# A third buffer for one-hot tiles, eight gathered rows later, and other steps for two blocks' picks

## The chip, the cores and the metric

The kernel runs on one core of a Trainium2 chip. The metric is the device time of one launch in microseconds; three runs of the kernel before gave 2902.71, 2904.64 and 2911.29 us, so its median is 2904.64 us. The profiled execution took 2901.28 us.

## The reference, cut to what matters

A sequence of 512 tokens of width 1024 goes through two mixing layers and a third block. The last part of that block is the expert layer that the change touches:

```
s = einsum('thpc,hpnc->thpn', q, sub_keys)          # 8 heads, two halves of 128 keys
v1, i1 = top_k(s[:, :, 0], 16);  v2, i2 = top_k(s[:, :, 1], 16)
top_s, pos = top_k(v1[..., :, None] + v2[..., None, :], 16)   # of 256 sums
idx = take_along_axis(cand_idx, pos);  g = softmax(top_s)     # cand_idx = i1 * 128 + i2
a = einsum('thkd,td->thk', u[idx], x);  w = gelu(a) * g
out = einsum('thk,thkd->td', w, v[idx])              # u, v: 16384 experts x 1024
```

Every token takes 8 x 16 = 128 of 16384 experts, each with its own row of u and of v. After it comes a small gated projection, and the output is stored.

## The kernel before, in words

The 512 tokens are four blocks of 128. The expert layer is computed in two ways at the same time.

**Blocks 0 and 1, gathered.** There are 256 "rows": row r is one expert per token. GpSimd gathers the row of u (512 KB for 128 tokens) into one of four buffers (L1903), VectorE multiplies it with XN, the block's normalised rows, and sums (row_dot, L2552), ScalarE makes gelu times the softmax weight of it (L1689, L1691), GpSimd gathers the row of v (L1912), and VectorE adds it, weighted, to X (row_add, L2564). row_add(r - 8) follows row_dot(r) on VectorE and waits for the weight of row r - 8. XN holds both blocks, 4 KB per partition each: XN[:, 0] at 196 KiB, XN[:, 1] at 200 KiB. XN[:, 1] is read from row 128 on.

**Blocks 2 and 3, dense.** A loop over 128 steps g (TILES), written out by hand, multiplies the 256 tokens with all experts, 128 at a time. In step g TensorE computes tile_products(g + 1) (L1216) from a STREAM tile that SyncE loads into a ring of three (L623); ScalarE takes gelu of the products (L1734, and L1732 for the part whose gates are known). The gates of a token are a 128 x 128 table, built four tokens at a time ("quads", 64 of them) in steps 82 to 126, one or two per step: VectorE writes one-hot tiles (quad_ones, L2612) into ONE, which has two buffers, at 12 and 204 KiB; ScalarE scales one half of each by the softmax (scale_quad, L1741, four instructions); TensorE multiplies the halves (build_quad, L1234) into one of three banks; ScalarE keeps the columns of later steps (keep_quad, L1748), and VectorE multiplies the earlier ones into the products (quad_gates, L2621). tile_gates(g) (L2628, VectorE) multiplies gelu(g) with the gates that were already kept. After step 127 follow 128 tile_sums on TensorE (L1244), with further STREAM tiles, while the rest of the gathered rows goes on.

**The order in a step.** VectorE: a share of the routing (top-16 searches, one-hot picks), the "ahead" quad_ones of step g + 1, tile_gates(g), rows up to rows_by(g), quad_gates of step g, then the "behind" quad_ones of step g + 1. ScalarE: gelu(g), scale of the ahead quads, row weights up to weighed_by(g), keep_quad of step g, scale of the behind quads. Which quads are ahead is told by ones_ahead (L108): those whose buffer the quads built before step g have left. rows_by (L114) is 46 + 3(g + 1)/5 up to step 82 (95 rows there), then one row in two steps (117 at step 127). The engines are tied by semaphores alone and each runs its own list in order, so VectorE may be several steps behind ScalarE.

**Picks.** The routing of block 2 ends in VectorE's step 39, that of block 3 in step 73 (PICKED_2, PICKED_3 less one); it ends with soft_start (L2529). ScalarE takes the exponential in its step PICKED + 5 (L1708), VectorE divides by the sum in its step PICKED + 6 (soft_end, L2533 to L2535), TensorE transposes the picks in its step PICKED + 8 (L1225), ScalarE copies them in step PICKED + 9 (L1713). All waits are by semaphore.

**Around the loop.** Before the STREAM tiles SyncE stores SCORES[1] and two blocks of X to memory (L609, L611). After step 127 ScalarE issues the load of SCORES[1] into KEPT (L1825), which VectorE needs for the next piece of routing.

Of the kernel before, what the change touches and what calls it, by code (L numbers as in the profile page):

```python
# [14 lines left out]
P = 128  # L15
# [34 lines left out]
TILES = 128  # L50
STREAM_RING = 3
PICKED_2, PICKED_3 = 40, 74
SOFT_AFTER, SOFT_END, TURNED, TURNED_COPY = 5, 6, 8, 9
QUAD_FROM = 82
DENSE_HEADS = (2, 3, 0, 1)
ARENA = 215360
SCALE128 = float(128 ** -0.5)
# [49 lines left out]

def ones_ahead(g):  # L108

    free = quads_by(g - 1) + 2  # L110
    return [q for q in quads_of(g + 1) if q < free], [q for q in quads_of(g + 1) if q >= free]


def rows_by(g):  # L114

    if g < 0:
        return 46
    if g <= QUAD_FROM:
        return 46 + (g + 1) * 3 // 5
    return rows_by(QUAD_FROM) + (g - QUAD_FROM) // 2  # L120


def row_place(r):
# [96 lines left out]
def program(nc, x, xT, mem, wstream, fmvec, rows, norm_rows, consts, levels, subkeys, pT, proj, peer_u, peer_v,  # L220
            experts, out):
    with ExitStack() as ctx:
# [23 lines left out]
        HROWN = at("HROWN", [P, P], 204)  # L246

        STREAM = [at(f"STREAM{i}", [P, D], kib) for i, kib in enumerate((24, 28, 8))]
        ONE = [at("ONE0", [P, 2, 4, P], 12), at("ONE1", [P, 2, 4, P], 204)]
        XTD = at("XTD", [P, KD, 2 * P], 16)  # L250
        KEPT = at("KEPT", [P, 2048], 16)
        GD = at("GD", [P, 256 * P], 32)
# [250 lines left out]
        scores_back = sem("scores_back")  # L503
        x_spilled = sem("x_spilled")
        x_back = sem("x_back")
        unit_in = sem("unit_in")
        unit_exp = sem("unit_exp")
        unit_picked = sem("unit_picked")
# [70 lines left out]
                self.n, self.off = base + times * per, 0  # L579

        scores_kept = nc.dram_tensor("scores_kept", [P, 2048], F32, kind="Internal").ap()
        x_kept = nc.dram_tensor("x_kept", [P, 2, D], F32, kind="Internal").ap()

        block = ctx.enter_context(nc.Block())
# [2 lines left out]
        @block.sync  # L587
        def _(sp):
            for k in range(KD):
                sp.dma_start(XT[:, k, :], xT[k * P:(k + 1) * P, :]).then_inc(first_loaded[k], 16)  # L590
                sp.dma_start(W[:, 0, k * T:(k + 1) * T], wstream[0][:, k * T:(k + 1) * T]
                             ).then_inc(first_loaded[k] if k < KD - 1 else slot_loaded[0], 16)
            sp.dma_start(mem_tm.rearrange("p (b d) -> p b d", b=2),
                         mem.rearrange("(b p) d -> p b d", p=P)).then_inc(loaded_mem, 16)
            sp.dma_start(W[:, 1, :], wstream[1]).then_inc(slot_loaded[1], 16)
            sp.dma_start(V[:, :], fmvec).then_inc(loaded_const, 16)
            sp.dma_start(C[:, :], consts).then_inc(loaded_const, 16)
            sp.dma_start(HROWN[:, :], norm_rows[640:768].partition_broadcast(P)).then_inc(loaded_const, 16)
            sp.dma_start(X[:, :, :], x.rearrange("(b p) d -> p b d", p=P)).then_inc(loaded_x, 16)

            n = SLOTS["ple"]
            with sp.Fori(1, n // 2) as i:
                for s in range(2):
                    sp.wait_ge(slot_used, i * 2 + s - 1)
                    sp.dma_start(W[:, s, :], wstream[ds(i * 2 + s, 1)].rearrange("a p n -> (a p) n")
                                 ).then_inc(slot_loaded[s], 16)

            sp.wait_ge(sk_ready, 4)
            sp.dma_start(scores_kept, SCORES[1]).then_inc(scores_out, 16)  # L609
            sp.wait_ge(h_ready, 4)  # L610
            sp.dma_start(x_kept, X[:, 2:4, :]).then_inc(x_spilled, 16)  # L611

            sp.wait_ge(bank_full, POS["xT_f2"] + 2)
            for m in range(2 * TILES):
                if m == 2:
                    sp.wait_ge(x_spilled, 16)
                if m >= STREAM_RING:
                    last = m - STREAM_RING
                    if last < TILES:
                        sp.wait_ge(a_full, last + 1)  # L620
                    else:
                        sp.wait_ge(v_used, last + 1 - TILES)
                sp.dma_start(STREAM[m % STREAM_RING][:, :], experts[m]).then_inc(streamed[m % STREAM_RING], 16)  # L623

            for i, b in enumerate(PLE_ORDER):
                for half in range(2):
                    cols = slice(half * T, (half + 1) * T)
                    sp.wait_ge(y_ready, 2 * i + half + 1)
                    sp.dma_start(out[0, b * P:(b + 1) * P, cols], xb(b)[:, cols]).then_inc(stored, 16)
            sp.wait_ge(stored, 16 * 2 * NB)  # L630
# [3 lines left out]
        def _(pe):  # L634
# [593 lines left out]
            def build_quad(q):  # L1228

                pe.wait_ge(quad_scaled, q + 1)  # L1230
                if q >= 3:
                    pe.wait_ge(quad_gated, q - 2)
                for i in range(4):
                    mm = pe.matmul(BUILD_BANK[q % 3][:, i * P:(i + 1) * P], ONE[q % 2][:, 1, i, :],  # L1234
                                   ONE[q % 2][:, 0, i, :], start=True, stop=True)
                mm.then_inc(built, 1)

            def tile_sums(i):
# [50 lines left out]
            for g in range(TILES):  # L1289
                if g + 1 < TILES:  # L1290
                    tile_products(g + 1)
                for b in (2, 3):
                    if g == (PICKED_2, PICKED_3)[b - 2] + TURNED:
                        picks_transposed(b)
                for q in quads_of(g):
                    build_quad(q)
# [24 lines left out]
        def _(act):  # L1321
# [415 lines left out]
            def scale_quad(q):  # L1737

                act.wait_ge(quad_hot, q + 1)
                for i in range(4):  # L1740
                    ins = act.activation(ONE[q % 2][:, 1, i, :], ONE[q % 2][:, 1, i, :], ACT.Copy,  # L1741
                                         scale=IT[:, 2, 4 * q + i:4 * q + i + 1])
                ins.then_inc(quad_scaled, 1)

# [61 lines left out]
            for g in range(TILES):  # L1806
                gelu(g)
                for b in (2, 3):
                    at_step = (PICKED_2, PICKED_3)[b - 2]
                    if g == at_step + SOFT_AFTER:  # L1810
                        exponentials(b)
                    if g == at_step + TURNED_COPY:
                        picks_copied(b)
                ahead, behind = ones_ahead(g)
                for q in ahead:
                    scale_quad(q)
                row_weights(weighed_by(g))
                for q in quads_of(g):
                    keep_quad(q, g)
                for q in behind:  # L1820
                    scale_quad(q)
            for r in range(rows_by(TILES - 1) - LAG, ROWS):
                if r == rows_by(TILES - 1):
                    act.wait_ge(a_full, TILES)
                    act.dma_start(KEPT[:, :], scores_kept).then_inc(scores_back, 16)  # L1825
                if r == rows_by(TILES - 1) + 64:
                    act.wait_ge(v_used, 68)
                    for n in range(2):
                        act.dma_start(PLE_W[n], wstream[SLOTS["ple"] + n]).then_inc(loaded_ple[n], 16)
                    act.dma_start(PROJ, proj).then_inc(loaded_proj, 16)  # L1830
                    act.dma_start(PLE_P, pT.rearrange("(k p) t -> p k t", p=P)).then_inc(loaded_proj, 16)
                    act.dma_start(XB, x_kept).then_inc(x_back, 16)
                if r == rows_by(TILES - 1) + 87:
                    ple_copies(0)
                    ple_roots(0)
                if r == rows_by(TILES - 1) + 93:
                    ple_sigmoid(0)
                if r == ROWS - 16:
                    ple_copies(1)
                    ple_copies(2)  # L1840
                if r == ROWS - 14:
                    ple_roots(1)
                    ple_roots(2)
                if r == ROWS - 9:
                    ple_sigmoid(1)
                row_weights(r + 1)
# [77 lines left out]
        def _(dve):  # L1924
# [621 lines left out]
            def row_dot(r):  # L2546
# [2 lines left out]
                dve.wait_ge(u_loaded[at], 16 * uses)  # L2549
                if r >= HELD:  # L2550
                    dve.wait_ge(weights, r - HELD + 1)
                dve.tensor_tensor_reduce(out=ROW_U[at][:, :], in0=ROW_U[at][:, :], in1=XN[:, r // P, :], scale=1.0,  # L2552
                                         scalar=0.0, op0=ALU.mult, op1=ALU.add,
                                         accum_out=DOT[:, r % HELD:r % HELD + 1]).then_inc(dots, 1)
# [50 lines left out]
            def quad_ones(q):  # L2605

                if q % 32 == 0:
                    dve.wait_ge(it_copied, q // 32 + 1)
                if q >= 2:
                    dve.wait_ge(built, q - 1)  # L2610
                wide = [P, 2, 4, P]
                dve.tensor_tensor(ONE[q % 2][:, :, :, :],  # L2612
                                  IOTA.rearrange("p (a t i) -> p a t i", a=1, t=1).broadcast_to(wide),
                                  IT[:, 0:2, 4 * q:4 * q + 4].rearrange("p a (t i) -> p a t i", i=1).broadcast_to(wide),
                                  ALU.is_equal).then_inc(quad_hot, 1)
# [45 lines left out]
            for g in range(TILES):  # L2661
                draw_to(route_quota(g))
                for b in (2, 3):
                    at_step = (PICKED_2, PICKED_3)[b - 2]
                    if g == at_step - 1:
                        while blocks_routed < b:
                            draw_to(drawn + 1)
                    if g == at_step + SOFT_END:
                        soft_end(b)
                ahead, behind = ones_ahead(g)  # L2670
                for q in ahead:
# [129 lines left out]
```

## Time and profile before

| what | value |
|---|---|
| profiled execution | 2901.28 us |
| its span | 2899.2 us |
| median of the runs | 2904.64 us |
| PE busy | 2726.3 us, 94% |
| DVE (VectorE) busy | 1789.2 us, 62% |
| ACT (ScalarE) busy | 765.6 us, 26% |
| POOL (GpSimd) busy | 798.4 us, 28% |
| mean transfer rate | 186 GB/s |
| chain that ended last | PE 68%, DVE 12%, DMA 9%, ACT 4% |

The span runs from the first to the last instruction of the profile. The busy share is a mean over the whole span; the chain that ended last is followed back from the last instruction, at each step to what released it. The loop of 128 steps lies between 1748 and 2310 us, the sums behind it. A number with an L is a line of the kernel before.

### The profile page before, as it was taken

What the parts mean: (1) busy time and instruction counts of PE and PEld (TensorE: products, weight loads), DVE (VectorE), ACT (ScalarE), POOL (GpSimd) and SP (SyncE); (2) the same over time, 40 slices, a digit from 0 to 9 for tenths busy, and PEclk for the clock granted to TensorE, in tenths of its full rate; (3) what the DMA queues carried; (4) which work ended last, traced back from release to release, by engine and by line L of the source; (5) the groups of instructions that cost most, each with busy time, mean ns of one, the idle gap of its engine ahead of it and who ended that gap; (6) DMA issues with size and microseconds to landing.
All of it is one profiled execution on the core that took longest, in us unless ns stands there. A gap on an engine that the chain in (4) does not pass through costs nothing.

```text
span 2899.2 us, 28503 instructions
## 1 busy us (share of the span) xinstructions
PE 2726.3 (94%) x9462; PEld 1577.3 (54%) x9462; DVE 1789.2 (62%) x3592; ACT 765.6 (26%) x2036; POOL 798.4 (28%) x601
## 2 busy tenths in 40 slices
PE   9999999999999979999999999979999899989986
PEld 4454454444565444446655678868888744434433
DVE  3998733007762222248851667999777687757876
ACT  1113420102331011345631332211444411101222
POOL 2830010000000000003310455444422265545664
PEclk9999999999999989999999999989999999999988
DMA  5131122121101121110022699988866699999996
GB/s 204 58 116 58 58 102 77 72 84 58 59 30 73 58 92 58 61 59 30 30 95 86 218 344 366 354 302 313 302 198 206 202 371 409 409 412 409 401 392 229
DMA packets 125475, 540.24 MB, mean 186 GB/s; under 512 B 13856, under 2 KB 14240, under 8 KB 117536
## 3 DMA queue, kind: packets, MB, share of 16 engines
q0 software_dynamic: 73728, 268.47, 24.8%
q1 hardware_dynamic: 49184, 253.82, 23.4%
q10 hardware_dynamic: 2432, 16.29, 1.5%
q8 instruction: 72, 1.18, 0.2%
q14 instruction: 59, 0.48, 0.0%
HBM read 534.33 MB, written 4.19 MB: 186 GB/s over the span
## 4 chain that ended last, share of the span: by engine, by line
PE 68%; DVE 12%; DMA 9%; ACT 4%; issue 4%; POOL 1%; DVEq 0%; ACTq 0%; SPq 0%; POOLq 0%
PE ps L652 17%; PE ps L1244 9%; DMA STREAM<-experts 8%; PE ps L1216 7%; PE ps L771 7%; PE ps L708 6%; PE ps L928 2%; PE ps L957 2%; PE ps L1140 2%; ACT ONE L1741 2%; PE ps L1128 2%; DVE X L2564 2%; DMA ROW_V<-peer_v,C 2%; DVE ONE L2612 1%; PE ps L753 1%
## 5 line engine op out<-in xcount | busy, mean ns | idle before, releaser
L652 PE MATMUL ps<-XT,W 128*128 128x512 f32 (+1 forms) x1216 | 471.8, 548 | 6.8 <-issue 4.5
L1244 PE MATMUL ps<-STREAM,GD 128*128 128x512 f32 x1024 | 455.1, 601 | 21.2 <-DMA STREAM<-experts 17.7
L1216 PE MATMUL ps<-XTD,STREAM 128*128 128x256 f32 x2048 | 457.9, 382 | 16.6 <-ACT GD L1734 8.6
L1216 PEld LDWEIGHTS ps<-XTD,STREAM 128*128 128x128 f32 x2048 | 386.9, 192 | 74.1 <-DMA STREAM<-experts 14.2
L1903 POOL DMA_INDIRECT ROW_U<-peer_u,C x208 | 260.1, 1250 | 398.7 <-DVE DOT L2552 377.9
L652 PEld LDWEIGHTS ps<-XT,W 128*128 128x128 f32 x1216 | 229.6, 190 | 248.0 <-issue 238.4
L1244 PEld LDWEIGHTS ps<-STREAM,GD 128*128 128x128 f32 x1024 | 190.2, 191 | 284.2 <-issue 199.8
L2564 DVE SCALAR_TENSOR_TENSOR X<-ROW_V,WEIGHT,X 128x1024 f32<-128x1024 f32 x208 | 267.3, 1285 | 92.9 <-DMA ROW_V<-peer_v,C 81.7
L2552 DVE CUSTOM_DVE_ANT_0 ROW_U<-ROW_U,XN 128x1024 f32<-128x1024 f32 x208 | 253.8, 1220 | 54.5 <-DMA ROW_U<-peer_u,C 53.0
L1912 POOL DMA_INDIRECT ROW_V<-peer_v,C x208 | 241.5, 1161 | 154.4 <-DVE X L2564 119.1
L771 PE MATMUL ps<-W,Y 128*128 128x512 f32 x512 | 221.8, 594 | 3.7 <-ACT H L1335 1.4
L708 PE MATMUL ps<-XT,W 128*128 128x512 f32 x448 | 217.0, 598 | 1.7 <-ACT G L1352 1.7
L1875 POOL COPY PR<-H 128x256 f32<-128x256 f32 x4 | 1.4, 392 | 730.8 <-DVE H L2201 730.8
L771 PEld LDWEIGHTS ps<-W,Y 128*128 128x128 f32 x512 | 96.6, 190 | 127.8 <-issue 123.9
L1975 DVE SCALAR_TENSOR_TENSOR Y<-H,V,Y x240 | 163.4, 763 | 0.0
L1689 ACT ACTIVATE ACTED<-DOT 128x1 f32<-128x1 f32 x256 | 50.4, 197 | 338.0 <-DVE DOT L2552 337.1
L1887 POOL TENSOR_TENSOR H<-H 128x256 f32<-128x256 f32 x56 | 51.7, 925 | 287.3 <-ACT H L1592 273.0
L1861 POOL TENSOR_TENSOR H<-H,SIG 128x512 f32 x12 | 108.0, 9003 | 78.0 <-ACT SIG L1412 74.5
L2085 DVE SCALAR_TENSOR_TENSOR X<-X,H 128x512 f32<-128x512 f32 x16 | 11.1, 691 | 183.7 <-ACT H L1335 183.7
L708 PEld LDWEIGHTS ps<-XT,W 128*128 128x128 f32 x448 | 79.3, 192 | 61.0 <-issue 56.6
L1741 ACT ACTIVATE ONE<-ONE,IT 128x128 f32<-128x128 f32 x256 | 81.6, 390 | 103.9 <-DVE ONE L2612 103.9
L1903 POOL DMA_INDIRECT EARLY_U<-peer_u,C x48 | 60.0, 1249 | 175.3 <-DVE C L2491 134.1
(353 smaller groups left out, 3619.5 us busy)
## 6 DMA issues: line engine op xcount, KB each, us to landing
STREAM<-experts SPq DMA_DIRECT2D x256, 512.0 KB, 6.8
W<-wstream SPq DMA_DIRECT2D x51, 2048.0 KB, 8.5
GD<-wstream ACTq DMA_DIRECT2D x2, 2048.0 KB, 15.6
ROW_U<-peer_u,C POOLq DMA_INDIRECT x208, 10.5
ROW_V<-peer_v,C POOLq DMA_INDIRECT x208, 10.6
XT<-xT SPq DMA_DIRECT2D x8, 256.0 KB, 5.6
W<-wstream SPq DMA_DIRECT2D x8, 256.0 KB, 6.0
X<-x SPq DMA_DIRECT2D x1, 2048.0 KB, 19.0
```

The costliest lines, as they stand in the source:

```text
L652: mm = pe.matmul(b[:, 0:rhs[k].shape[-1]], w[:, k, m * P:(m + 1) * P], rhs[k], start=(k == 0), stop=(k == KD - 1))
L708: mm = pe.matmul(FILL_BANK[j % 2][:, :], w[:, k, m * P:(m + 1) * P], XT[:, k, :], start=(k == 0), stop=(k == KD - 1))
L771: mm = pe.matmul(ps[pos % 4][:, :], Y[:, (j * KD + k) * T + b * P:(j * KD + k) * T + (b + 1) * P], w[:, k, :], start=(j == 0 and k == 0), ...
L1216: mm = pe.matmul(UP_BANK[g % 2][:, 0:256], u[:, k, :], XTD[:, k, :], start=(k == 0), stop=(k == KD - 1))
L1244: mm = pe.matmul(acc(b, n)[:, :], GD[:, i * 256 + b * P:i * 256 + (b + 1) * P], STREAM[m % STREAM_RING][:, n * T:(n + 1) * T], start=(i == ...
L1741: ins = act.activation(ONE[q % 2][:, 1, i, :], ONE[q % 2][:, 1, i, :], ACT.Copy, scale=IT[:, 2, 4 * q + i:4 * q + i + 1])
L1861: pool.tensor_tensor(hrow(i * 4 + j, TAPS - 1, T), hrow(i * 4 + j, TAPS - 1, T), SIG[:, j, :], ALU.mult).then_inc(glu_done, 1)
L1903: pool.indirect_dma_start(ROW_U[at][:, :], None, peer_u, bass.IndirectOffsetOnAxis(ap=IDX[:, r:r + 1], axis=0)).then_inc(u_loaded[at], 16)
L1912: pool.indirect_dma_start(ROW_V[at][:, :], None, peer_v, bass.IndirectOffsetOnAxis(ap=IDX[:, r:r + 1], axis=0)).then_inc(v_loaded[at], 16)
L1975: ins = dve.scalar_tensor_tensor(yt(c), hrow(c, k, T), V[:, ds(c * TAPS + (FM["conv_w"] + k), 1)], yt(c), ALU.mult, ALU.add)
L2552: dve.tensor_tensor_reduce(out=ROW_U[at][:, :], in0=ROW_U[at][:, :], in1=XN[:, r // P, :], scale=1.0, scalar=0.0, op0=ALU.mult, op1=ALU.ad ...
L2564: dve.scalar_tensor_tensor(X[:, b, :], ROW_V[at][:, :], WEIGHT[:, r % HELD:r % HELD + 1], X[:, b, :], ALU.mult, ALU.add).then_inc(v_added, 1)
```

## The change

XN[:, 1], idle until row 128, is lent to the quads as a third buffer: it is stored to memory before the loop and loaded again behind it, ahead of KEPT on the same queue. The ring of ONE has three slots, ones_ahead counts with three. rows_by gives 46 + (g + 1)/2 up to step 82 (87 there) and two rows in three steps behind it (117 at step 127 again). For block 2 the exponential moves from ScalarE's step 45 to 48, the division from VectorE's step 46 to 43, the transposes from 48 to 51 and the copy from 49 to 52; for block 3 only the transposes and the copy move, by one step, to 83 and 84.

```diff
-SOFT_AFTER, SOFT_END, TURNED, TURNED_COPY = 5, 6, 8, 9
+SOFT_AFTER, SOFT_END, TURNED, TURNED_COPY = (8, 5), (3, 6), (11, 9), (12, 10)
+ONE_RING = 3
 def ones_ahead(g):
-    free = quads_by(g - 1) + 2
+    free = quads_by(g - 1) + ONE_RING
 def rows_by(g):
     if g <= QUAD_FROM:
-        return 46 + (g + 1) * 3 // 5
-    return rows_by(QUAD_FROM) + (g - QUAD_FROM) // 2
+        return 46 + (g + 1) // 2
+    return rows_by(QUAD_FROM) + (g - QUAD_FROM) * 2 // 3
-        ONE = [at("ONE0", [P, 2, 4, P], 12), at("ONE1", [P, 2, 4, P], 204)]
+        ONE = [at("ONE0", [P, 2, 4, P], 12), at("ONE1", [P, 2, 4, P], 204), at("ONE2", [P, 2, 4, P], 200)]
+        xn_kept = nc.dram_tensor("xn_kept", [P, D], F32, kind="Internal").ap()
             sp.dma_start(scores_kept, SCORES[1]).then_inc(scores_out, 16)
+            sp.wait_ge(rows_gained, 2)
+            sp.wait_ge(bank_full, POS["xT_f1"] + 2)
+            sp.dma_start(xn_kept, XN[:, 1, :]).then_inc(xn_stored, 16)
             sp.wait_ge(h_ready, 4)
             sp.dma_start(x_kept, X[:, 2:4, :]).then_inc(x_spilled, 16)
# ScalarE, behind step 127
                     act.wait_ge(a_full, TILES)
+                    act.wait_ge(built, 64)
+                    act.dma_start(XN[:, 1, :], xn_kept).then_inc(xn_back, 16)
                     act.dma_start(KEPT[:, :], scores_kept).then_inc(scores_back, 16)
# VectorE, row_dot and quad_ones
+                if r == P:
+                    dve.wait_ge(xn_back, 16)
-                if q >= 2:
-                    dve.wait_ge(built, q - 1)
+                if q >= ONE_RING:
+                    dve.wait_ge(built, q - ONE_RING + 1)
+                if q == ONE_RING - 1:
+                    dve.wait_ge(xn_stored, 16)
```

The other lines replace `q % 2` by `q % ONE_RING` and the four constants by their entry for the block.

## Rows read from the trace of the kernel before

**Rows 1.** Windows: length, PE, PEld, DVE, ACT, POOL busy; clock, DMA share, GB/s.

```profile
1850.00:2050.00 200.00, 178.29 (x799) 153.74 (x798) 192.08 (x560) 37.61 (x121) 93.54 (x73) 0.95 0.89 321
2071.00:2308.00 237.00, 217.98 (x1232) 192.37 (x1230) 171.01 (x239) 115.71 (x457) 62.41 (x44) 1.00 0.63 207
2308.00:2720.00 412.00, 393.96 (x895) 166.15 (x896) 296.50 (x535) 67.53 (x232) 216.32 (x196) 0.99 1.01 398
```

**Rows 2.** Waits of 1748 to 2082: us in total, times, longest.

```profile
ACT C L1708 <- DVE C L2529: 11.6, 1, 11.6
...
PE ps L1225 <- DVE C L2535: 9.7, 1, 9.7
...
PE ps L1216 <- ACT GD L1734: 8.6, 1, 8.6
```

**Rows 3.** Windows of L1734 alone: us, ACT busy (count), clock, DMA share, GB/s.

```profile
1751.77:1915.62 163.85, 17.25 (x45) 1.00 0.95 360
1915.62:1959.86 44.24, 3.57 (x7) 0.77 0.77 271
1959.86:2058.88 99.02, 10.76 (x28) 1.00 0.89 313
```

**Rows 4.** Window of all engines behind the first wait of TensorE.

```profile
1930.00:1931.10 1.10, 0.00 (x0) 0.03 (x1) 1.10 (x3) 1.06 (x4) 0.77 (x1) 0.50 0.40 164
```

**Rows 5.** L2529 by its source line; timeline of ACT.

```profile
L2529 DVE TENSOR_TENSOR C<-C x2: 291/292/293, 1928.6 to 2050.8; 128x128 f32<-128x128 f32 x2
...
2059.28 1.28 ACT L1708 ACT_TABLE_LOAD   x1
```

**Rows 6.** L2628 (tile_gates) by source: first, last start; timeline, steps 99 to 104.

```profile
L2628 DVE TENSOR_TENSOR GD<-GD,V x23: 157/293/471, 2077.4 to 2309.6; 128x4 f32<-128x4 f32 x1, 128x16 f32<-128x16 f32 x1, 128x28 f32<-128x28 f32 x1, 128x36 f32<-128x36 f32 x1
...
2162.98 0.26 DVE L2628 TENSOR_TENSOR GD<-GD,V 128x96 f32<-128x96 f32 x1 [0.53 <-ACT GD L1734]
...
2167.67 0.26 DVE L2628 TENSOR_TENSOR GD<-GD,C 128x100 f32<-128x100 f32 x1 [1.67 <-ACT GD L1734]
...
2174.05 0.27 DVE L2628 TENSOR_TENSOR GD<-GD,V 128x108 f32<-128x108 f32 x1 [0.54 <-ACT GD L1734]
...
2176.99 0.27 DVE L2628 TENSOR_TENSOR GD<-GD,C 128x112 f32<-128x112 f32 x1
...
2183.47 0.28 DVE L2628 TENSOR_TENSOR GD<-GD,V 128x116 f32<-128x116 f32 x1 [1.67 <-ACT GD L1734]
...
2188.20 0.29 DVE L2628 TENSOR_TENSOR GD<-GD,C 128x124 f32<-128x124 f32 x1 [0.54 <-ACT GD L1734]
```

**Rows 7.** Timeline of steps 106 to 108, all engines: start, us, engine, line.

```profile
2200.29 0.29 ACT L1691 ACTIVATE WEIGHT<-ACTED,C 128x1 f32<-128x1 f32 x1
...
2200.68 1.33 DVE L2564 SCALAR_TENSOR_TENSOR X<-ROW_V,WEIGHT,X 128x1024 f32<-128x1024 f32 x1 [0.20 <-issue]
...
2204.87 0.21 ACT L1748 ACTIVATE GD<-ps 128x80 f32<-128x80 f32 x1
2205.11 0.60 DVE L2621 TENSOR_TENSOR GD<-GD,ps 128x432 f32<-128x432 f32 x1 [1.25 <-ACT GD L1748]
...
2208.75 1.22 DVE L2552 CUSTOM_DVE_ANT_0 ROW_U<-ROW_U,XN 128x1024 f32<-128x1024 f32 x1
...
2211.09 1.12 DVE L2621 TENSOR_TENSOR GD<-GD,ps 128x436 f32<-128x436 f32 x2
2212.12 2.36 DVE L2612 TENSOR_TENSOR ONE<-C,IT 128x1024 f32<-128x1024 f32 x2
...
2213.38 1.28 ACT L1741 ACTIVATE ONE<-ONE,IT 128x128 f32<-128x128 f32 x4 [3.64 <-DVE ONE L2612]
```

**Rows 8.** Behind the loop: the KEPT wait, its landing, two windows.

```profile
DVE TOPV L2436 <- DMA KEPT<-scores_kept: 9.1, 1, 9.1
...
DMA to landing us min/median/max: 8.4/8.4/8.4
...
2310.00:2315.00 5.00, 4.85 (x12) 2.25 (x13) 0.05 (x1) 0.89 (x5) 0.53 (x1) 1.00 0.92 291
```

More of the change, by code:

```diff
@@ L505, in program @@
         x_back = sem("x_back")
+        xn_stored = sem("xn_stored")
+        xn_back = sem("xn_back")
         unit_in = sem("unit_in")
@@ L1233, in build_quad @@
                 for i in range(4):
-                    mm = pe.matmul(BUILD_BANK[q % 3][:, i * P:(i + 1) * P], ONE[q % 2][:, 1, i, :],
-                                   ONE[q % 2][:, 0, i, :], start=True, stop=True)
+                    mm = pe.matmul(BUILD_BANK[q % 3][:, i * P:(i + 1) * P], ONE[q % ONE_RING][:, 1, i, :],
+                                   ONE[q % ONE_RING][:, 0, i, :], start=True, stop=True)
                 mm.then_inc(built, 1)
@@ L1292, in _ @@
                 for b in (2, 3):
-                    if g == (PICKED_2, PICKED_3)[b - 2] + TURNED:
+                    if g == (PICKED_2, PICKED_3)[b - 2] + TURNED[b - 2]:
                         picks_transposed(b)
@@ L1740, in scale_quad @@
                 for i in range(4):
-                    ins = act.activation(ONE[q % 2][:, 1, i, :], ONE[q % 2][:, 1, i, :], ACT.Copy,
+                    ins = act.activation(ONE[q % ONE_RING][:, 1, i, :], ONE[q % ONE_RING][:, 1, i, :], ACT.Copy,
                                          scale=IT[:, 2, 4 * q + i:4 * q + i + 1])
@@ L1809, in _ @@
                     at_step = (PICKED_2, PICKED_3)[b - 2]
-                    if g == at_step + SOFT_AFTER:
+                    if g == at_step + SOFT_AFTER[b - 2]:
                         exponentials(b)
-                    if g == at_step + TURNED_COPY:
+                    if g == at_step + TURNED_COPY[b - 2]:
                         picks_copied(b)
@@ L2608, in quad_ones @@
                     dve.wait_ge(it_copied, q // 32 + 1)
-                if q >= 2:
-                    dve.wait_ge(built, q - 1)
+                if q >= ONE_RING:
+                    dve.wait_ge(built, q - ONE_RING + 1)
+                if q == ONE_RING - 1:
+                    dve.wait_ge(xn_stored, 16)
                 wide = [P, 2, 4, P]
-                dve.tensor_tensor(ONE[q % 2][:, :, :, :],
+                dve.tensor_tensor(ONE[q % ONE_RING][:, :, :, :],
                                   IOTA.rearrange("p (a t i) -> p a t i", a=1, t=1).broadcast_to(wide),
@@ L2667, in _ @@
                             draw_to(drawn + 1)
-                    if g == at_step + SOFT_END:
+                    if g == at_step + SOFT_END[b - 2]:
                         soft_end(b)
```

## The prediction

> **What bounds the kernel now.** I read first the windows over the three stretches that the change touches, then the waits of the loop's first part, the gelu of each step, and the timeline of a few quad steps. Steps 0 to 81 run at TensorE's pace: 45 steps took 163.85 us (3.64 each), 28 later ones 99.02 us (3.54 each) [rows 3]. VectorE is busy beside it for 192.1 of 200 us [rows 1], nearly without a pause, and behind ScalarE: it ends block 2's routing, its step 39, at 1928.6 [rows 5], when ScalarE, which reached step 45 at 1915.62, is due in step 48. So ScalarE waits 11.6 us for the exponential's input and TensorE 8.6 us behind it; TensorE then waits 9.7 us for the divided picks [rows 2]. In steps 82 to 127 no engine is full (TensorE 218.0 of 237 us, VectorE 171.0) and TensorE's 19 us of idle time come from a ring VectorE, ScalarE, VectorE: tile_gates often starts only after a wait for gelu, 0.53 or 1.67 us, which on ScalarE stands behind a scaling [rows 6]. Behind the loop the DMA engines are full, share 1.01 at 398 GB/s [rows 1]: what is won before them moves all of that stretch forward, as no byte of it goes away and the same 139 rows are left at step 127.
>
> **The picks of block 2.** From gelu(45) to gelu(51) passed 44.24 us (the seven activations of that window are six gelus and a table load) [rows 3]. Six undisturbed steps are 6 x 3.64 = 21.8 us, so the two waits cost 22.4. After: rows_by(39) is 66 instead of 70, and a row is 1.22 us of dot and about 1.28 us of add [rows 7], 2.5 together. VectorE was full, so its step 39 ends 10 us sooner, near 1919; ScalarE reaches step 48 at 1915.62 + 3 x 3.64 = 1926.5 and finds its input. VectorE's step 43 would begin near 1926 and wait about 2 us for that exponential (table load 1.28 us [rows 5], then 0.3); the picks are divided by 1929.5, and TensorE wants them in step 51, near 1937. Both waits go: -22.4. I take -22, since some of it had been given back: behind the waits the STREAM ring was full. What is late next is block 3: soft_start came at 2050.8 [rows 5]; seven rows fewer by step 73 (83 against 90) and the 2 us lost make it 2050.8 - 17.5 + 2 = 2035.3, and ScalarE is due in step 79 at 1915.62 + 34 x 3.54 = 2036. A tie; a stall of up to 3 us is kept for the range. Bounds: all gone and fewer waits for STREAM tiles, since rows bring less traffic, -26; the wait moved to block 3, -22 + 14 = -8 (below, as a rival). The later transposes of block 3 have their picks either way: nothing.
>
> The row behind the first wait has the granted clock at 0.50 [rows 4], that is 1.2 of 2.4 GHz, after TensorE had stood still for 8.6 us. The Trainium skill (TensorE: Matmul & The Clock Gate, Part 1) has the array's clock halved when it has been idle and back after sustained work; the trace agrees. By the idle times alone (8.6 + 9.7) the picks would be worth 18.3 us, and the sum 4 us less; the step count, which holds the slow clock too, decides.
>
> **The quad steps.** Per step one or two quads are built, n, and m are built in the next. Steps 83 to 126 run from 2077.4 to 2309.6, 232.2 us [rows 6]. The new rule makes all quad_ones ahead: before, with n = 2, none was. VectorE's step is then: ones (m of them), tile_gates, perhaps a row, gates (n). ScalarE's scalings come right behind the ones, and row weight and keep_quad stand in line behind them. Counted from the first ones: scaling starts at 1.26 and takes 1.28 a quad, row_add starts 0.2 + 0.39 later and takes 1.25, or without a row keep_quad and its gap take 0.24; then gates, 1.12 for two with 1.03 to the next ones, so 0.52 for one [rows 7]. That gives for (n, m):
> (1, 2) with a row 1.26 + 2.56 + 0.59 + 1.25 + 0.52 = 6.2 us, without 4.6;
> (2, 1) with a row 1.26 + 1.28 + 0.59 + 1.25 + 1.03 = 5.4, without 3.8;
> (1, 1) with a row 4.9, without 3.3.
> By the formulas of the code there are 12, 7, 12, 6, 4 and 2 of these, and step 126 with no ones, 3.9: 74.4 + 32.2 + 64.8 + 22.8 + 19.6 + 6.6 + 3.9 = 224.3 us. Before, steps 99 to 103 show 4.7 for (1, 2) without a row, 6.4 for (2, 1) with, 2.9 for (1, 1) without, 6.5 for (1, 2) with, 4.7 for (2, 1) without [rows 6]: the third buffer shortens the steps by the wait for gelu, and eight more rows take back most of it. So -232.2 + 224.3 = -8. TensorE does not stop this: a quad scaled in step g is wanted a whole step later, and its own floor, 19 us under the present time [rows 1], is below the ring. The exponential of gathered unit 3 (two table loads of 1.28 us and an activation), which stood at step 81, moves to step 94: +3 in one place and -3 in the other. Bounds: -19 (TensorE never waits) and, if no step gets shorter and a row costs what it does now (6.4 - 4.7 = 1.7 us in a (2, 1) step), +8 x 1.7 = +14, with the exponential +3.
>
> **XN stored and loaded.** The store is one more issue on SyncE's queue, 512 KB between two stores that were there, before the first STREAM tiles; the queries of blocks 2 and 3 run meanwhile on weights issued earlier. I take 0, bounds 0 and +2 (the time of 512 KB beside other traffic, doubled), since the x_kept store and STREAM tile 2 behind it come later. The load stands ahead of KEPT on ScalarE's queue. KEPT, 1 MB, took 8.4 us beside the streams, 125 GB/s, and VectorE waited 9.1 us [rows 8]; another half MB in front makes that about 4.2 us longer. The DMA engines bound this stretch, so what counts is their time: 0.524 MB at 398 GB/s is 1.3 us, and for 4.2 us they move 291 GB/s [rows 8] instead of 398, 1.1 us. Sum +2.4; bounds +1.3 (bytes alone) and +5.5 (VectorE's whole wait on top). XN is needed at row 128, eleven rows on: no wait. The Trainium skill (DMA: Bandwidth & Descriptors, Queues, rings and completion order) says that each DMA engine takes the descriptors of one ring in order and goes round between queues: by it KEPT can't overtake XN, and this part of the change can only cost. No run here shows it yet.
>
> **Sum.** 2901.3 - 22 - 8 + 2.4 = 2873.7 us for the profiled execution; it lies 3.4 us below the median of the runs (2904.64 - 2901.28), so 2877 us.
>
> **Rivals.**
> A, TensorE sets the pace in the quad steps: 2904.6 - 22 - 19 + 2.4 = 2866. For it: VectorE would be busy 171 + 20 of 218 us. Against: the serial order on ScalarE above.
> B, the third buffer gains just what eight rows cost: 2904.6 - 22 + 2.4 = 2885.
> C, the wait for picks moves to block 3: were VectorE's early part held by transfers and not by its own work, soft_start(3) would stay at 2050.8 while ScalarE comes at 2036, 14 us: 2904.6 - 8 - 8 + 2.4 = 2891. Against: 192 of 200 us busy.
> D, rows are paid in full in the quad steps: 2904.6 - 22 + 17 + 2.4 = 2902, no change. For it: row_add is in the ring by its weight. Against: the waits for gelu, which nothing keeps.
> E, slower: VectorE becomes the bound of the loop. Its time then counts wherever it is spent: the eight rows at 2.5 us are 20 in the quad steps and the exponential 3, and block 3's picks come no earlier, +14 of the 22: 2904.6 - 8 + 23 + 2.4 = 2922. It decides once VectorE's pauses in the quad steps, 237 - 171 = 66 us now, are fixed waits and not slack.
>
> **Chances.** Own forecast 0.42 (2868 to 2884), A 0.16, B 0.17, C 0.08, D 0.10, E 0.07. The first four are faster by over 0.3% (about 9 us, which is what a measurement can tell from no change): 0.83; D 0.10 the same; E 0.07 slower. The range takes in A's point and C, leaves out D and E and the far side of A: 2863 to 2897.
>
> **What would show it.** ScalarE's wait for L2529 and TensorE's for L2535 gone, and no granted clock below 1 near step 48; gelu(51) about 22 us sooner. No wait of tile_gates for gelu in the quad steps, and these some 224 us long, with the ring still through ScalarE's scaling. VectorE's wait for KEPT near 13 us. A wait of ScalarE for block 3's L2529 of over 3 us, or quad steps over 232 us, would make it wrong; so would a stretch behind the loop that lengthens by what the loop wins.

## The result, and the profile after

The changed kernel took 2868.72 us (five runs, 2865.92 to 2872.80) against 2904.64 us; the ratio is 0.9871 with the interval 0.9860 to 0.9882. That is 35.9 us less, where 27.6 had been forecast (2877). Its profiled execution took 2865.92 us with a span of 2863.8. By the stages that the prediction used:

| stretch, us | before | after | difference | forecast |
|---|---|---|---|---|
| start to gelu(0) | 1751.8 | 1753.9 | +2.1 | 0 |
| gelu(0) to gelu(79) | 307.1 | 283.1 | -24.0 | -22 |
| gelu(79) to tile_gates(83) | 18.6 | 17.7 | -0.9 | 0 |
| tile_gates(83) to (127) | 232.1 | 217.3 | -14.9 | -8 |
| behind the loop | 589.6 | 591.8 | +2.2 | +2.4 |

The forecasts 0 and -8 in the middle leave out the -3 and +3 that the prediction booked for the exponential of gathered unit 3. Gelu(g) is the start of the gelu of step g, counted from the rows as before. The 2.1 us at the start are no work of the change: the store of XN is issued at 1716.4, when SyncE's earlier issues are already as late, and the kernels below, whose program up to there differs in nothing but that store, start the loop between 1750.5 and 1756.9 us, with the store (1750.5 to 1755.7) no later than without it (1751.3 to 1756.9).

The first part of the loop varies by some us from kernel to kernel even where its code does not differ, and this bears on the second line of the table. The eight kernels below that share the changed picks and rows up to step 73 (e4 to e8, e10 to e12) have 285.4 to 288.9 us from gelu(0) to gelu(79); the changed kernel's 283.1 is the lowest of the nine. Against the 307.1 of before that is a gain of 18 to 24 us, and the -24.0 is its favourable end. Steps 45 to 51, where the waits were, are steadier: 21.8 us here and 21.3 to 23.2 in those eight, against 44.24.

The windows of the changed kernel: length, PE, PEld, DVE, ACT, POOL busy, granted clock, DMA share, GB/s. They are steps 45 to 51, the quad steps, and the stretch behind.

```profile
1916.50:1938.30 21.80, 21.30 (x97) 18.36 (x98) 21.17 (x63) 6.33 (x15) 8.71 (x7) 1.00 0.89 309
2050.00:2272.00 222.00, 215.81 (x1223) 191.57 (x1221) 183.66 (x260) 119.22 (x480) 60.19 (x58) 1.00 0.75 252
2272.00:2685.00 413.00, 395.92 (x897) 166.21 (x898) 298.35 (x538) 65.80 (x222) 221.01 (x197) 0.99 1.02 402
```

Six steps took 21.8 us, where [rows 3] had 44.24 at a clock of 0.77; the clock is 1.00 now. The waits of [rows 2] for the picks are gone. L2529 is L2538 here; by its source line the two soft_starts come at

```profile
L2538 DVE TENSOR_TENSOR C<-C x2: 291/292/292, 1920.7 to 2033.6; 128x128 f32<-128x128 f32 x2
```

8 and 17 us sooner than in [rows 5]. ScalarE reached its steps 48 and 79 after 1927 and at 2037.0 and waited for neither. VectorE waited for nothing at the division of block 2 but 0.2 us.

The waits of the quad steps of the changed kernel (2050 to 2272):

```profile
ACT ONE L1748 <- DVE ONE L2625: 97.9, 43, 3.2
...
DVE GD L2634 <- ACT GD L1755: 22.3, 16, 2.6
DVE X L2575 <- issue: 16.3, 27, 3.5
PEld ps L1241 <- ACT ONE L1748: 8.5, 18, 1.1
```

These are the two waits of the kernel before (2077 to 2310) to set beside them:

```profile
DVE GD L2628 <- ACT GD L1734: 41.3, 37, 1.7
...
PE ps L1234 <- ACT ONE L1741: 18.1, 15, 2.0
```

tile_gates' wait for gelu, of which [rows 6] shows single ones, is not in the list of the changed kernel at all, and TensorE's wait for scaled halves (L1241 now) has fallen to 2.3 us. In their place stands row_add (L2575), which waits 27 times, 16.3 us in all, with nothing that the profile names: its weight, which ScalarE makes behind the scalings. The timeline of VectorE and ScalarE, steps 104 to 108:

```profile
2158.88 2.35 DVE L2625 TENSOR_TENSOR ONE<-C,IT 128x1024 f32<-128x1024 f32 x2
...
2163.25 1.22 DVE L2625 TENSOR_TENSOR ONE<-C,IT 128x1024 f32<-128x1024 f32 x1
...
2165.91 0.29 ACT L1698 ACTIVATE WEIGHT<-ACTED,C 128x1 f32<-128x1 f32 x1
...
2166.29 1.28 DVE L2575 SCALAR_TENSOR_TENSOR X<-ROW_V,WEIGHT,X 128x1024 f32<-128x1024 f32 x1 [0.48 <-issue]
...
2168.51 1.22 DVE L2625 TENSOR_TENSOR ONE<-C,IT 128x1024 f32<-128x1024 f32 x1
...
2173.26 2.35 DVE L2625 TENSOR_TENSOR ONE<-C,IT 128x1024 f32<-128x1024 f32 x2
...
2174.51 2.44 ACT L1748 ACTIVATE ONE<-ONE,IT 128x128 f32<-128x128 f32 x8 [2.59 <-DVE ONE L2625]
...
2177.63 1.22 DVE L2625 TENSOR_TENSOR ONE<-C,IT 128x1024 f32<-128x1024 f32 x1
```

From ones to ones the steps last 4.37 us for (1, 2) without a row, 5.26 for (2, 1) with one, 4.75 for (1, 1) with one, 4.37 again. The prediction had 4.6, 5.4, 4.9 and 4.6.

### The profile page after: what moved, and what is told of

Same layout as the page of the kernel before. It is cut to its first block and busy times, and to the rows that moved or that the text cites. A ratio compares the mean times of both kernels' runs of the same rounds, so it can differ in the third digit from the quotient of the medians.

```text
span 2863.8 us, 28505 instructions
## 1 busy us (share of the span) xinstructions
PE 2722.6 (95%) x9462; PEld 1575.1 (55%) x9462; DVE 1786.1 (62%) x3592; ACT 763.1 (27%) x2036; POOL 776.3 (27%) x601
## 5 line engine op out<-in xcount | busy, mean ns | idle before, releaser
L2575 DVE SCALAR_TENSOR_TENSOR X<-ROW_V,WEIGHT,X 128x1024 f32<-128x1024 f32 x208 | 267.0, 1284 | 99.9 <-DMA ROW_V<-peer_v,C 81.6
L1921 POOL DMA_INDIRECT ROW_V<-peer_v,C x208 | 224.5, 1079 | 163.8 <-DVE X L2575 132.1
```

The lines of the kernel that those rows point to most:

```text
L1921: pool.indirect_dma_start(ROW_V[at][:, :], None, peer_v, bass.IndirectOffsetOnAxis(ap=IDX[:, r:r + 1], axis=0)).then_inc(v_loaded[at], 16)
L2575: dve.scalar_tensor_tensor(X[:, b, :], ROW_V[at][:, :], WEIGHT[:, r % HELD:r % HELD + 1], X[:, b, :], ALU.mult, ALU.add).then_inc(v_added, 1)
```

## The experiments

All are compared with the kernel before on the same chip, whose median there was 2906.99 us beside e1 to e4, 2906.40 beside e5 to e8 and 2907.55 beside e10 to e12; the ratios, with their intervals, are to it and need not equal the quotient of two medians. The stages come from one profiled execution of each kernel, which can lie off its median: 8.2 us above it in e1, 7.4 in e12, 5.1 in e3, 4.0 below it in e10. The length of the quad steps is read from one row of each profile, tile_gates by source: min/median/max ns, then first and last start. The edits are shown condensed.

**The parts, alone and without one.**

```diff
# e1: SOFT_AFTER, SOFT_END, TURNED, TURNED_COPY alone      # e2: rows_by alone
+SOFT_AFTER, ... = (8, 5), (3, 6), (11, 9), (12, 10)       +46 + (g + 1) // 2;  ... * 2 // 3
# e3: ONE_RING = 3 with its store and load alone           # e4: e1 and e2 together, two buffers
```

> The kernel before with the picks' new steps alone (old rows, two ONE buffers). Theory 1 (steps and later rows must go together): block 2's two waits go, but VectorE keeps its pace, so soft_start(3) stays near 2051 to 2053 while ScalarE is due in step 79 near 2036: a wait of some 15 us there. Quad steps stay 232 us. Total -22 + 16, about 2899 us. Theory 2 (the new steps do it all, VectorE's load does not matter): no wait at block 3, about 2882 us.

It took 2902.90 us, ratio 0.9982 (0.9971 to 0.9994). The wait went from block 2 to block 3. ScalarE's waits in it, by source line:

```profile
L1708 ACT ACT_TABLE_LOAD  x2: 1283/1283/1283, 1925.5 to 2042.7; - x2
L1708 ACT ACTIVATE C<-C x2: 309/309/309, 1933.8 to 2053.3; 128x128 f32<-128x128 f32 x2
...
  DVE C L2529: 16.4, 2
```

From the end of each table load to its exponential it waited 7.0 us at block 2 and 9.3 at block 3. Gelu(0) to gelu(79) fell by 17.4 us, and gelu(79) to tile_gates(83) grew from 18.6 to 35.0. Theory 1 holds in kind: the new steps by themselves are worth about 4 us. Its sizes were off, as no wait was expected at block 2 and some 15 us at block 3; VectorE reached block 2's soft_start at 1933.5, 5 us later than in the kernel before.

> The kernel before with the later rows alone. Theory 1: soft_start(2) comes 8 to 10 us sooner, which ScalarE's step 45 still misses by 3 to 5 us; the divided picks (VectorE's step 46, near 1939) come some 10 us after TensorE's step 48 wants them; so about half of the 22 us is won. In the quad steps eight more rows at 1.7 us each lengthen 232 to about 245 us. Total near 2906 us. Theory 2 (rows cost nothing there): quad steps 232 us, total near 2892 us.

It took 2906.47 us, ratio 1.000 (0.999 to 1.001). ScalarE no longer waited for the exponential's input (3 to 5 us were expected), TensorE waited 3.8 us for the divided picks (10 were expected), gelu(0) to gelu(79) was 290.0 us, 17 less than before, and the quad steps were 246.9, 15 more. What the later rows win in the first part they lose in the second. It also shows that most of the gain at the picks comes from the later rows: 17 us with the old steps of the picks, where both changes together give 18 to 24.

> The changed kernel with the picks' steps and the rows as before: the third buffer with its store and load alone. Block 2's waits stay (22 us). Theory R (a ring of VectorE and ScalarE sets the pace of the quad steps after the change): with eight rows fewer the ring falls under TensorE's floor, quad steps 213 to 215 us, thus 2 to 4 us less than the 217.3 of the change. Theory P (TensorE sets the pace after the change): the same 217 us. Behind the loop +2 us. Total 2887 to 2891 us.

It took 2884.05 us, ratio 0.9922 (0.9903 to 0.9941).

```profile
L2641 DVE TENSOR_TENSOR GD<-GD,V x23: 153/284/465, 2089.1 to 2295.5; 128x4 f32<-128x4 f32 x1, 128x16 f32<-128x16 f32 x1, 128x28 f32<-128x28 f32 x1, 128x36 f32<-128x36 f32 x1
```

206.4 us. The third buffer alone is worth 26 us in the quad steps with the old rows. And 206.4 is less than 217.3: the eight rows still cost 10.9 us, so TensorE does not set the pace in the changed kernel. It also lies under the floor of 213 us that the prediction took from TensorE's idle time; in theory R's favour, and a miss of its number. The total is below the expected 2887 to 2891 as well: by its ratio this one part gives some 23 of the 36 us.

> The changed kernel with two ONE buffers, no store and load of XN: picks' steps and rows as changed. Theory 1: no waits for picks, gelu(79) as in the change; quad steps 232 + 13 = 245 us since every row costs 1.7 us in the old ring; behind the loop 2 us shorter than in the change. Total 2868.7 + 28 - 2, about 2894 us. Rival (the later rows are free in the quad steps whatever the ring): quad steps 232 us, about 2882 us.

It took 2896.98 us, ratio 0.9980 (0.9966 to 0.9994).

```profile
L2628 DVE TENSOR_TENSOR GD<-GD,V x23: 155/291/468, 2054.1 to 2301.0; 128x4 f32<-128x4 f32 x1, 128x16 f32<-128x16 f32 x1, 128x28 f32<-128x28 f32 x1, 128x36 f32<-128x36 f32 x1
```

246.9 us, and gelu(0) to gelu(79) 285.6 without the third buffer. The changed kernel without it keeps only 6 to 10 us of the 36 (by the ratio and by the medians). The four kernels make a table of the quad steps: 232.1 and 246.9 us with two buffers (old and new rows), 206.4 and 217.3 with three. A row costs (246.9 - 232.1) / 8 = 1.85 us in the old ring and (217.3 - 206.4) / 8 = 1.36 in the new. The 1.36 is a mean that TensorE's share in e3 holds down (see e7): in the changed kernel's own steps of one kind, with and without a row, the difference is 5.92 - 4.42 = 1.50 and 5.26 - 3.73 = 1.53 us.

**The order of the two loads.**

```diff
-dma_start(XN[:, 1, :], xn_kept); dma_start(KEPT, scores_kept)
+dma_start(KEPT, scores_kept); dma_start(XN[:, 1, :], xn_kept)
```

> The changed kernel with the two loads behind the loop in the other order: KEPT first, XN behind it. If the queue keeps its order, VectorE's wait for KEPT falls from 8.3 us by some 2 us (without the load of XN it was 5.9 us, in the kernel with two ONE buffers and the changed rows and picks), and row 128 finds XN anyway. Theory 1 (the DMA engines bound this stretch, so only the bytes count): the time stays within 2 us of the change. Rival (VectorE's wait counts in full): 2 to 3 us faster.

It took 2869.65 us, ratio 0.9871 (0.9848 to 0.9893), which can't be told from the change; the stretch behind took 591.9 us against 591.8. VectorE's wait, after and here:

```profile
DVE TOPV L2445 <- DMA KEPT<-scores_kept: 8.3, 1, 8.3
```

```profile
DVE TOPV L2445 <- DMA KEPT<-scores_kept: 5.6, 1, 5.6
```

In this pair the load in front makes the wait 2.7 us longer. That is one pair, and the wait varies as much by itself: without the load it was 9.1 us before, 8.4 in e1, 9.0 in e2, 5.9 in e4 and 6.5 in e12; with the load in front, at the same row, 8.3 in the change, 10.9 in e3, 10.3 in e7 and 9.4 in e10. Nor does the total decide between the two theories: they lie 2 to 3 us apart, and the interval reaches some 6 us to either side.

**What the ring runs through.**

```diff
-                for i in range(4):   # scale_quad
+                for i in range(1):
```

> The changed kernel in which ScalarE scales one of the four tokens of a quad; the softmax weights of the other three are left out. It takes 0.9 us of 1.28 from every scaling. Theory R (the ring goes through the scaling, by row_add's wait for its weight and by keep_quad): quad steps fall from 217.3 us to TensorE's floor, which the third buffer with the old rows showed at 206 us, or near it (205 to 208). Theory P (TensorE already sets the pace at 217 us): they stay at 216 to 217 us.

It took 2861.47 us, a single run.

```profile
L2641 DVE TENSOR_TENSOR GD<-GD,V x23: 157/286/418, 2058.0 to 2264.3; 128x4 f32<-128x4 f32 x1, 128x16 f32<-128x16 f32 x1, 128x28 f32<-128x28 f32 x1, 128x36 f32<-128x36 f32 x1
```

```profile
2058.00:2264.00 206.00, 205.48 (x1197) 187.45 (x1195) 179.98 (x258) 68.95 (x274) 88.30 (x58) 1.00 0.77 256
```

206.3 us with all 30 rows, the same as e3 with 22: two ways to the same length, with TensorE busy for 205.5 of 206 us here and 205.3 of 206.5 there. This is TensorE's floor. Shortening ScalarE's scalings alone gives 11 us, so the ring through them set the pace. (Its stretch behind was 595.0 us, 3 more than the change.)

**More rows in the loop.** In both kernels the two loads behind the loop stay at row 117.

```diff
# e6                                      # e8: 7 rows in 9 steps from 74 to 82
-... (g - QUAD_FROM) * 2 // 3             +    if g < PICKED_3: return 46 + (g + 1) // 2
+... (g - QUAD_FROM) * 3 // 4             +    if g <= QUAD_FROM: return 83 + (g + 1 - PICKED_3) * 7 // 9
```

> The changed kernel with three rows in four steps behind step 82 instead of two in three: 120 rows at step 127, three fewer behind the loop (the loads stay at row 117). Theory R (a ring of VectorE and ScalarE sets the pace of the quad steps): they grow by 3 x 1.4 = 4 us to about 221.5 us (eight rows cost 217.3 - 206.4 = 10.9 us), the stretch behind shrinks by 3 x 1 MB at 398 GB/s = 7.9 us: net -4 us, about 2865 us. Theory P (TensorE sets it): 217 us, net -8 us.

It took 2869.61 us, ratio 0.9875 (0.9853 to 0.9897): no gain that can be measured. The quad steps took 223.3 us, +6.0 for three rows where 4 had been expected, and the stretch behind 586.3, -5.5; by this profile a row there is worth 1.8 us and not 2.6.

> The changed kernel with seven rows in nine steps from step 74 to 82 (90 rows there instead of 87), two in three behind it as in the change: 120 rows at step 127 too, but the three more rows stand where VectorE has done its routing and no quad is built. Quad steps stay 217 us, steps 74 to 82 grow by 0 to 3 us, behind the loop -7.9 us: net -5 to -8 us, about 2862 us. If VectorE is still behind there, block 3's picks come late and TensorE waits for them in step 83 by up to 5 us; then no better than the version with 120 rows by three in four.

It took 2868.26 us, ratio 0.9866 (0.9848 to 0.9884): no gain that can be measured either. The quad steps stayed at 217.0 us, but steps 79 to 83 grew by 3.3 and the stretch behind fell by 3.1 only.

**The weights one step ahead.** Since row_add's wait was the new one, ScalarE was made to weigh the row of the next step in this one; its dot is long done.

```diff
-... rows_by(g - 3 if g < 60 else g) - LAG
+... rows_by(g - 3 if g < 60 else g if g < QUAD_FROM else g + 1) - LAG
```

> The changed kernel with ScalarE's row weights one step ahead behind step 82 (weighed_by takes rows_by(g + 1)): the dot of that row was made eight rows before, so nothing waits for it. Theory R (row_add waits for its weight behind the scalings, 16.3 us over 27 rows in the change): the waits go, the quad steps fall from 217.3 us to near TensorE's floor of 206.3 us, say 207 to 209 us, and all of it moves forward: about 2860 us, 8 to 10 us under the change. Rival (keep_quad behind the scalings is what counts): quad steps 214 to 217 us, time as the change.

It took 2864.37 us, ratio 0.9858 (0.9841 to 0.9875).

```profile
L2641 DVE TENSOR_TENSOR GD<-GD,V x23: 154/284/467, 2055.0 to 2264.8; 128x4 f32<-128x4 f32 x1, 128x16 f32<-128x16 f32 x1, 128x28 f32<-128x28 f32 x1, 128x36 f32<-128x36 f32 x1
```

209.8 us, 7.5 less, and row_add's wait is gone, so it was the weight. Of the whole it is 4.4 us where 8 to 10 were expected, and the interval overlaps that of the change. VectorE's waits in these steps are now for keep_quad alone:

```profile
DVE GD L2634 <- ACT GD L1755: 30.8, 21, 3.0
```

> As before, with 120 rows at step 127 by three rows in four steps. Theory R: with the weight's wait gone a row costs its own 2.5 us where VectorE is full and nothing where TensorE is: quad steps 208 to 213 us; behind the loop 3 to 5 us less than in the change. About 2857 us. If 120 rows again give back all they win, 2860 us.

It took 2858.64 us (2856.12 to 2861.93), ratio 0.9836 (0.9821 to 0.9851), and its interval is clear of the change's (0.9860 to 0.9882). The quad steps took 210.9 us and the stretch behind 589.1, 2.7 less than in the change.

> Two ONE buffers, changed rows and picks, and the weights one step ahead: tells whether the third buffer is still needed once the weights are early. In the old ring the scalings ahead of the weight were one or none, and tile_gates' wait for gelu stood behind the scaling of the step before: theory R says that the quad steps stay long, 241 to 246 us (246.9 without the early weights), so about 2893 us. Rival (the weight was the whole of it): 215 to 225 us, about 2870 us.

It took 2889.90 us, ratio 0.9938 (0.9922 to 0.9955), quad steps 244.7 us, and tile_gates waits for gelu as it did before:

```profile
DVE GD L2628 <- ACT GD L1734: 41.2, 37, 1.7
```

In the quad steps early weights give 2 us with two buffers, so what the third buffer takes away is the other wait, that of tile_gates. The whole fell by more: 7 us by the medians of e4 and e12, whose intervals are apart. The two profiled executions (2894.41 and 2897.34 us) don't show where, and this stays open; e10 is still 25 us below e12.

## Why the prediction was right, and where its sizes were off

**The whole.** Faster, and in the range, with 8.3 us more won than forecast. In the profiles it is 7.8 us: 6.9 from the quad steps, 2.0 from steps 0 to 79 and 0.9 from the steps between, less 2.1 for the later start. 2868.72 lies just inside the prediction's own band from 2868.

**What bounds the kernel.** Right in what it was used for: all that was won before step 127 came through, as the stretch behind kept its length (589.6 and 591.8 us). That the DMA engines are full behind the loop was read from its first 412 us; in the last 179 us of the kernel before they moved 327 GB/s with a share of 0.85, and 326 with 0.85 in the last 178 of the changed one.

**Picks.** Right in mechanism. Steps 45 to 51 gave 44.24 - 21.8 = 22.4 us, just the price that the prediction took; the rest of the -24.0 over steps 0 to 79 is luck, as the spread above shows. That price was the step count, not the 18.3 us of idle time: with 21.3 to 23.2 us for these steps in the other kernels, 21 to 23 us are won in each. soft_start(2) came at 1920.7 where 1919 was forecast, soft_start(3) came at 2033.6 where 2035.3 was forecast, ScalarE at 2037.0 where 2036; the tie went well by 3 us. e1 shows rival C's wait at block 3, though not from C's cause: what differs there from the changed kernel is that VectorE has seven more rows to do by step 73. e4 has the gain without the third buffer. The price beyond the idle time, 22.4 - 18.3 = 4.1 us, goes with a granted clock of 0.77 in [rows 3] against the 1.00 of the window above; no run here shows how much of it is the clock's.

**Quad steps.** The forecast of the ring was right, the size was not: 224 us were forecast, 217.3 measured, so that 14.9 us were won and not 8. "Eight more rows take back most of it" was too much: by e3 the third buffer gains 25.7 us and the rows take back 10.9. The failing terms are the durations of a step, each a little long: two scalings in a row take 2.44 us, not 2.56, and a (1, 2) step with a row 5.92 instead of 6.2, a (2, 1) step 5.26 instead of 5.4 (means of twelve each). Over the 42 steps that can be measured from ones to ones this makes 7.4 us, the two ends 2.5, and the exponential of unit 3 puts 2.9 back: 224.3 - 7.4 - 2.5 + 2.9 = 217.3. The exponential was booked as -3 and +3; step 94 did take 7.67 us instead of 4.75, but where it had stood only 0.9 us went.

**Rival A** forecast 2866, nearer to the measured time than the forecast, and is still wrong: by e3 and e7 TensorE could do these steps in 206 us, and it was not what held them at 217. Its floor of 213 came from 19 us of idle time in a profile whose matmul ends are modelled, while the floor is 206. Rival B, at 2885, took the rows to eat all that the buffer gains, which e3 rules out. Rival D's price of a row, 1.7 us, is near the 1.85 that e4 shows for the old ring, but the new ring charges less and the wait for gelu went. Rival E needed 2.5 us for a row and a wait at block 3: no run shows the 2.5, and e1 has such a wait only with the old rows.

**XN.** +2.2 for +2.4, but the agreement is worth nothing. With the load and 117 rows the stretch behind took 591.4 to 595.0 us (e3, e5, e7, e10 and the change), without it 589.6 to 599.1 (before, e1, e2, e4 and e12), so no run shows a price of the load at all. VectorE's wait for KEPT "near 13 us" did not come: it was 8.3 us, and 10.9 at most in the kernels with the load in front. The term that was off is the 4.2 us that another half MB was to add to the wait; the one pair gives 2.7.

**What stays open.** Why three rows fewer shorten the stretch behind by 2.7 to 5.5 us and not by the 7.9 of their bytes; part of this is the spread of some 3 us that the stretch has by itself. In e6 its later part moves 323 GB/s with a DMA share of 0.84, much as in the change, so it is not full to the end; which order of the last rows would fill it was not tried. Nor is it shown why e1's stretch behind took 599 us; its profiled execution took 8.2 us more than its median.

## What to carry to other kernels

A wait that a lagging engine causes is not removed by asking later: the new steps alone moved it from block 2 to block 3, and only less work on that engine, put where it has room, made it go. A further buffer in a ring pays by taking a serial piece out of the circle; price it by writing down one step of the circle that will be left, and look there for the next wait, here the weight of a row that queued behind scalings. The length of a stage less TensorE's idle time was no floor for TensorE here (213 us, where 206 can be reached): take the floor from a run in which the other engines are shortened. And set a stage against the same stage of kernels that don't differ in it before you call a difference of 2 us a success.

## What the runs showed of the hardware

Eight scalings of 128x128 in a row take 2.44 us, two groups of four apart 1.28 each. TensorE's busy time in the quad steps was 210.8 of 217 us in the changed kernel (2055 to 2272) and 205.5 of 206 in e7 for the same matmuls, so 97% busy still left 11 us to win.
